# Masked attentions of a fused decoder: division moved ahead of the turn, products with stationary values, scores in two sets of PSUM banks

## What is computed

```python
def fox_attention(hn, w_q, w_o, k, v, c_bhs):          # 16 heads of 64
    """Forgetting attention: logit[t,s] = q_t.k_s/sqrt(d) + c[t] - c[s], s<=t."""
    ...
        s = jnp.where(causal, s + bias, NEG_BIG)
        pr = jax.nn.softmax(s, axis=-1)
        return jnp.einsum("bhqk,bkhd->bqhd", pr.astype(v.dtype), v)
    ...
    return o @ w_o
def moba_attention(q, k, v):                           # 8 heads of 64
    ...
        s_own = (jnp.einsum("bhqd,bhkd->bhqk", qi, k_own) * scale
                 - slopes[..., None] * dist_own)
    ...
        scores = jnp.concatenate([s_sel.reshape(...), s_own], axis=-1)
        p = jax.nn.softmax(scores, axis=-1).astype(v.dtype)
```

## Time and profile before

| | us |
|---|---|
| median of 3 runs | 2239.92 (2239.6 to 2240.91) |
| the profiled execution's own time | 2240.7 |
| its span, first to last instruction | 2238.9 |
| busy: TensorE, VectorE, GpSimd, ScalarE | 2132.1, 1025.5, 936.6, 808.5 |
| mean granted TensorE clock | 0.981 |

### The profile page before, as it was taken

The page is one execution under the profiler, slowest core; times in us unless marked ns, Lnnn a source line. Parts: engine busy times, 40 slices in busy tenths (PEclk is TensorE's granted clock), DMA queues, the critical chain, the costliest instruction groups (busy, mean ns, idle before and its releaser), DMA issues.

```text
span 2238.9 us, 27199 instructions
## 1 busy us (share of the span) xinstructions
PE 2132.1 (95%) x10072; PEld 1750.2 (78%) x10072; DVE 1025.5 (46%) x1632; ACT 808.5 (36%) x1214; POOL 936.6 (42%) x435
## 2 busy tenths in 40 slices
PE   7977999999999988999999998999998999999997
PEld 6765888888878966788888876887877788888885
DVE  7995523122364345352232366248333346354353
ACT  6745422222352156332222354224244243222231
POOL 5974444444444300354444432343331434444441
PEclk9988999999999999999999999999999999999998
DMA  4321332232222310332222221222211222322221
GB/s 183 135 101 58 125 119 94 94 108 90 102 77 94 114 48 30 113 113 94 94 94 94 94 94 40 97 94 76 94 57 39 77 93 95 112 95 94 94 94 57
DMA packets 32204, 205.31 MB, mean 92 GB/s; under 512 B 4448, under 2 KB 4576, under 8 KB 9072
## 3 DMA queue, kind: packets, MB, share of 16 engines
q1 hardware_dynamic: 31824, 199.87, 25.5%
q10 hardware_dynamic: 288, 4.19, 0.5%
HBM read 197.73 MB, written 6.32 MB: 91 GB/s over the span
## 4 chain that ended last, share of the span: by engine, by line
PE 84%; DVE 9%; issue 3%; POOL 2%; ACT 2%; DMA 0%; DVEq 0%; ACTq 0%; POOLq 0%
PE gp L530 26%; PE gp L532 26%; PE gp L531 26%; PE gp L718 2%; DVE ms L1213 2%; PE ms L760 2%; POOL pool_sum L456 1%; PE ms L705 1%; DVE xc L1213 1%; DVE T L1210 1%; DVE U L1683 1%; PE ms L762 0%; DVE T L1565 0%; PE ms L656 0%; PE ms L596 0%
## 5 line engine op out<-in xcount | busy, mean ns | idle before, releaser
L433 POOL TENSOR_TENSOR w_lo<-raw,w_hi 128x1024 fp32r<-128x1024 f32 x350 | 846.6, 2421 | 1198.2 <-ACT w_hi L848 1180.7
L530 PE MATMUL gp<-a_hi,w_hi 128*128 128x512 f32 x1440 | 568.2, 395 | 20.4 <-DVE a_lo L1213 13.1
L531 PE MATMUL gp<-a_lo,w_hi 128*128 128x512 f32 x1440 | 564.2, 392 | 0.0
L532 PE MATMUL gp<-a_hi,w_lo 128*128 128x512 f32 x1440 | 564.1, 392 | 0.0
L848 ACT ACTIVATE w_hi<-raw 128x1024 fp32r<-128x1024 f32 x349 | 365.6, 1051 | 513.4 <-PE gp L532 512.3
L530 PE MATMUL gp<-b_hi,w_hi 128*128 128x512 f32 x1184 | 463.4, 391 | 10.2 <-DVE b_lo L1210 8.4
L531 PE MATMUL gp<-b_lo,w_hi 128*128 128x512 f32 (+1 forms) x1216 | 471.7, 388 | 0.0
L532 PE MATMUL gp<-b_hi,w_lo 128*128 128x512 f32 x1184 | 461.6, 390 | 0.0
L530 PEld LDWEIGHTS gp<-a_hi,w_hi 128*128 128x128 f32 x1440 | 272.7, 189 | 80.8 <-issue 14.8
L531 PEld LDWEIGHTS gp<-a_lo,w_hi 128*128 128x128 f32 x1440 | 272.6, 189 | 58.2 <-issue 1.7
L532 PEld LDWEIGHTS gp<-a_hi,w_lo 128*128 128x128 f32 x1440 | 272.6, 189 | 57.2
(11 more groups left out here) (263 smaller groups left out, 1944.1 us busy)
## 6 DMA issues: line engine op xcount, KB each, us to landing
raw<-w_hbm SPq DMA_DIRECT2D x176, 1024.0 KB, 4.8
proj_scratch<-kT ACTq DMA_DIRECT2D x2, 2048.0 KB, 6.6
fbias<-negc_scratch SPq DMA_DIRECT2D x16, 256.0 KB, 3.5
h<-x_hbm SPq DMA_DIRECT2D x4, 512.0 KB, 7.3
u_pad<-proj_scratch SPq DMA_DIRECT2D x1, 2048.0 KB, 9.7
big<-proj_scratch SPq DMA_DIRECT2D x1, 2048.0 KB, 8.6
out_hbm<-h SPq DMA_DIRECT2D x4, 512.0 KB, 2.7
mem_raw<-mem_hbm SPq DMA_DIRECT2D x1, 1024.0 KB, 12.3
```

What stands on the lines that cost most here:

```text
L433: g.tensor_tensor(at(w_lo), src, f32(at(w_hi)), ALU.subtract).then_inc(w_lo_done, 1)
L530: pe.matmul(o, wh, xh, start=start, stop=False)
L531: pe.matmul(o, wh, xl, start=False, stop=False)
L532: return pe.matmul(o, wl, xh, start=False, stop=stop)
```

## The change

In the masked attentions a pair i takes the place of the step as the grain of TensorE's order: scores of pair i, turns of pair i - 3, products of pair i - 4. Scores go to `ms[:, 0:2]` and `gp[:, 0:2]` in turn, so that they wait for the biases of the pair before the last. The weights have eight places, `prob_of`. VectorE takes both reciprocals of a pair in one instruction, between the pair's two biases, and GpSimd divides the weights by their sums before they are turned. ScalarE copies the first head's turned weights, VectorE the second's. In the products the values are stationary (64 columns) and the turned weights move (128 columns); the heads write partitions 0 to 63 and 64 to 127 of `gp[:, 2 + j % 2]`. The output so stands in its final orientation: the turn of the output and `o_sb` fall away here. TensorE no longer waits for the last remainder behind the attention; `gemm(wo)` has its own waits by k, and `branch(1)` waits before its third slab. In `mob` the wait for banks is reduced to two banks, before the second pair. GpSimd's divides stand in its queue ahead of the slabs of the next gemm, in `mob` with the later two bias products between them. The rest of the diff, left out, is new semaphore counts (`pt`, `pv`, `o`) for the cross attention, which keeps its order.

```diff
@@ -240,6 +240,8 @@
         big = u_pad[:, :, TAPS - 1:]
         bigs, proj_sb = (big, big1), kT
         prob, probT = T, (U[:, 1, :], acc_sq, sqb[:, 0, :], sqb[:, 1, :])
+        prob_of = (T[:, 2, 3 * P:], T[:, 3, 3 * P:], U[:, 0, 0:2 * P], U[:, 0, 2 * P:],
+                   T[:, 2, 0:3 * P], T[:, 3, 0:3 * P], T[:, 0, :], T[:, 1, :])
...
@@ -461,6 +463,13 @@
...
+            def divide(at, s):
+                r, w = s % 8, (s % 8 // 2 + 1) * P
+                g.wait_ge(sum_inv, at["step"] + s + 1)
+                p = prob_of[r][:, 0:w]
+                g.tensor_scalar(p, p, rinv[:, r:r + 1], None, ALU.mult).then_inc(weighted, 1)
...
@@ -477,7 +486,10 @@
             g.wait_ge(hg_done, gate[0]["hg"] + 8)
             g.memset(f32(wf_hi[:]), 0.0).then_inc(wf_zero, 1)
             g.memset(f32(wf_lo[:]), 0.0).then_inc(wf_zero, 1)
-            slabs(gq["slab"] + AHEAD, br[2]["slab"] + AHEAD)
+            slabs(gq["slab"] + AHEAD, wo["slab"] + AHEAD)
+            for s in range(64):
+                divide(fox, s)
+            slabs(wo["slab"] + AHEAD, br[2]["slab"] + AHEAD)
...
@@ -503,8 +515,10 @@
             mob_bias(1)
             for a in range(AHEAD):
                 slab(Pos(br[1]["slab"] + a))
-            mob_bias(2)
-            mob_bias(3)
+            for s in range(32):
+                divide(mob, s)
+                if s in (9, 17):
+                    mob_bias(s // 8 + 1)
             slabs(br[1]["slab"] + AHEAD, ffn2["slab"])
...
-            def head_scores(queries, keys):
-                def scores(j, s):
...
+            def head_attention(at, n, queries, keys, values, before):
...
+                t0, N = at["step"], 4 * n
+                def S_(i):
+                    j, qb = divmod(i, 4)
+                    w, bank = (qb + 1) * P, (ms, gp)[i % 2]
+                    if i == 1:
+                        for c in range(2):
+                            wait_evac(pe, before, c)
+                    if i >= 2:
+                        pe.wait_ge(biased, t0 + 2 * i - 2)
                     for hh in range(2):
                         r = slice(64 * hh, 64 * hh + 64)
-                        pe.matmul(ms[:, hh, 0:w], queries[r, j, qb * P:qb * P + P], keys[r, j, 0:w], start=True, stop=False)
+                        pe.matmul(bank[:, hh, 0:w], queries[r, j, qb * P:qb * P + P], keys[r, j, 0:w], start=True, stop=False)
                     for hh in range(2):
-                        pe.matmul(ms[:, hh, qb * P:w], identb[:], tri[:], start=False, stop=True).then_inc(scored, 1)
-                return scores
-            def head_v(t):
-                def v_of(j, s, kb):
-                    return t[:, kb, j * P + 64 * (s % 2):j * P + 64 * (s % 2) + 64]
-                return v_of
-            attention(fox, 8, biased, [1, 1, 2, 2, 3, 3, 4, 4], head_scores(qT, kT), head_v(v_s), 64, 2, 4)
+                        pe.matmul(bank[:, hh, qb * P:w], identb[:], tri[:], start=False, stop=True).then_inc(scored, 1)
+                def T_(i):
+                    for hh in range(2):
+                        s = 2 * i + hh
+                        pe.wait_ge(weighted, at["weighted"] + s + 1)
+                        if i:
+                            pe.wait_ge((pt_copied, pt_copied2)[hh], at[("pt", "pt2")[hh]] + i)
+                        for kb in range(i % 4 + 1):
+                            m = pe.transpose(ms[:, 2 + hh, kb * P:kb * P + P], prob_of[s % 8][:, kb * P:kb * P + P], ident[:])
+                        m.then_inc(transposed, 1)
+                def V_(i):
+                    j, qb = divmod(i, 4)
+                    pe.wait_ge(pt_copied, at["pt"] + i + 1)
+                    pe.wait_ge(pt_copied2, at["pt2"] + i + 1)
+                    if qb == 0 and j >= 2:
+                        pe.wait_ge(lo_done, at["split"] + j - 1)
+                    for kb in range(qb + 1):
+                        for hh in range(2):
+                            c = j * P + 64 * hh
+                            m = pe.matmul(gp[64 * hh:64 * hh + 64, 2 + j % 2, qb * P:qb * P + P], values[:, kb, c:c + 64],
+                                          probT[(2 * i + hh) % 4][:, kb * P:kb * P + P], start=(kb == 0), stop=(kb == qb),
+                                          skip_group_check=True)
+                    m.then_inc(pv_done, 1)
+                for i in range(N + 4):
+                    if i < N:
+                        S_(i)
+                    if 3 <= i < N + 3:
+                        T_(i - 3)
+                    if i >= 4:
+                        V_(i - 4)
+            head_attention(fox, 8, qT, kT, v_s, Pos(gv["blk"] + 12))
...
-            def branch(n, k0, ysplit, kn):
+            def branch(n, k0, ysplit, kn, late=4):
                 at = br[n]
                 for half in range(2):
                     sl, bl = at["slab"] + 6 * half, at["blk"] + 8 * half
                     for s in range(4):
+                        if s == late and not half:
+                            pe.wait_ge(lo_done, ysplit + kn)
                         slab_ws(Pos(sl + s), Pos(bl + s), A)
                     pe.wait_ge(lo_done, ysplit + kn)
                     for s in range(2):
...
             branch(0, 0, lru["split"], 4)
-            for c in range(4):
-                wait_evac(pe, Pos(br[0]["blk"] + 12), c)
-            attention(mob, 4, biased, [1, 1, 2, 2, 3, 3, 4, 4], head_scores(qm, km), head_v(vm), 64, 2, 4)
-            branch(1, 4, mob["split"], 4)
+            head_attention(mob, 4, qm, km, vm, Pos(br[0]["blk"] + 12))
+            branch(1, 4, mob["split"], 4, late=2)
...
-            def head_exp(s):
...
+            def head_attention(at, X, k0, n):
+                t0, N = at["step"], 4 * n
+                def E_(s):
+                    w = (s % 8 // 2 + 1) * P
+                    act.wait_ge(biased, t0 + s + 1)
+                    p = prob_of[s % 8][:, 0:w]
+                    act.activation(p, p, ACT.Exp, scale=-1.0, bias=nmax[:, s % 8:s % 8 + 1], accum_out=rsum[:, s % 8:s % 8 + 1]
+                                   ).then_inc(exped, 1)
+                def C_(i):
+                    w = (i % 4 + 1) * P
+                    act.wait_ge(transposed, t0 + 2 * i + 1)
+                    if i >= 2:
+                        act.wait_ge(pv_done, at["pv"] + i - 1)
+                    act.activation(probT[2 * i % 4][:, 0:w], ms[:, 2, 0:w], ACT.Copy).then_inc(pt_copied, 1)
+                def H_(j):
+                    act.wait_ge(pv_done, at["pv"] + 4 * (j + 1))
+                    act.activation(X[0][:, k0 + j], gp[:, 2 + j % 2], ACT.Copy).then_inc(hi_done, 1)
+                for i in range(N + 3):
+                    if i >= 3:
+                        C_(i - 3)
+                    if i < N:
+                        E_(2 * i)
+                        E_(2 * i + 1)
+                    if i >= 8 and i % 4 == 0:
+                        H_(i // 4 - 2)
+                H_(n - 1)
+            head_attention(fox, A, 0, 8)
...
-            attention(mob, B, 4, 4, 8, head_exp, causal, STATS, 4)
+            head_attention(mob, B, 4, 4)
...
-            def head_bias(b_of, ready):
-                def bias(j, s):
-                    qb, hh = s // 2, s % 2
+            def head_attention(at, X, k0, n, bias_of, ready):
+                t0, N = at["step"], 4 * n
+                def B_(s):
+                    j, qb, hh = s // 8, s % 8 // 2, s % 2
+                    w = (qb + 1) * P
                     if qb == 0:
                         ready(2 * j + hh)
-                    w = (qb + 1) * P
+                    v.wait_ge(scored, t0 + s + 1)
+                    if s >= 8:
+                        v.wait_ge(transposed, t0 + s - 7)
                     v.sem_inc(step_open, 1)
-                    return v.tensor_tensor_reduce(prob[:, s % 4, 0:w], ms[:, hh, 0:w], b_of(2 * j + hh, qb, w), -1.0, 3e38,
-                                                  ALU.add, ALU.min, nmax[:, s:s + 1])
-                return bias
-            def head_out(s):
-                return s // 2, 64 * (s % 2)
-            attention(fox, A, 0, 8, 8,
-                      head_bias(lambda r, qb, w: fbias[:, r % 4, 0:w], lambda r: v.wait_ge(bias_ready[r % 4], 16 * (r // 4 + 1))),
-                      64, head_out, STATS, 4)
+                    v.tensor_tensor_reduce(prob_of[s % 8][:, 0:w], (ms, gp)[s // 2 % 2][:, hh, 0:w], bias_of(2 * j + hh, qb, w), -1.0, 3e38,
+                                           ALU.add, ALU.min, nmax[:, s % 8:s % 8 + 1]).then_inc(biased, 1)
+                def R_(i):
+                    r = 2 * i % 8
+                    v.wait_ge(exped, t0 + 2 * i + 2)
+                    v.reciprocal(rinv[:, r:r + 2], rsum[:, r:r + 2]).then_inc(sum_inv, 2)
+                def C_(i):
+                    w = (i % 4 + 1) * P
+                    v.wait_ge(transposed, t0 + 2 * i + 2)
+                    if i >= 2:
+                        v.wait_ge(pv_done, at["pv"] + i - 1)
```

(61 more changed lines are left out.)

## The result

The changed kernel takes 2201.31 us (median of 4 runs, 2198.37 to 2202.81), the kernel before 2240.36 beside it: ratio 0.9826, 95% interval 0.9812 to 0.984, so 39 us less. The profiled execution of after is the fastest of its four, 2198.37 us with a span of 2196.6, against 2238.9 before: 42.3 less.

What follows compares the result with a forecast made beforehand. TensorE was taken as the bound, busy 95%, with order and waits costing 2.2 of each 12.87 us attention unit and products 4.5. First attention -28.1, second -15.6, together -43.7 from 2240.7, less 0.8 for the median: 2196 us, range 2187 to 2217.

Steps and rivals of the forecast that it cites:

- the forecast's own case: Whole kernel: products side by side and the change working as meant, 2187 to 2204 us, chance 0.60.
- Products side by side: Masked attentions' products: both heads' column halves stream together, 0.21 a pair of calls, 2.1 us a unit.
- The rival of products in sequence: Masked attentions' products: column halves run one after the other, units of 11.0, 2214 us; chance 0.25.
- TensorE's own work: A unit of two heads, four pairs: scores, masks, turns, products and switches sum to 8.7 us; residue for late hand-overs 0.2.
- VectorE's queue: In a unit: the copy behind both biases holds the next turns, 512 pair 2.95 instead of 2.5, unit 9.2.
- the division on GpSimd: Eight divides a unit: 0.61 to 1.29 for 512 columns, 3.4 to 6.9 us a unit, covered by the lag.
- Divides at the upper end would not lengthen it: In the attention units: even 6.9 us of GpSimd divides would leave the unit at 9.4 us.
- 2.1 us inside that lag: Second attention: two bias products of 1.04 in GpSimd's queue fit in the three pairs' lag (6 us or more).
- the last divides hide behind VectorE's queue: End of both attentions: divides done at 5.6, VectorE's copy only at 6.3; last scores to last products 8.8 us.
- The start: Both attentions: fourth scores at 3.2 us in the first, 4.0 in the second, plus 1.0 each for lost clock.
- The clock behind `mob`: Gemm behind the second attention: granted clock 0.87 over 13 us returns to 1.00, 1.7 us gained.
- The rival of a falling clock: In the attentions: turns and short products with more stops lose the granted clock, 2276 us; chance 0.05.

Runs made afterwards that it cites:

- cheap divides: The changed kernel with GpSimd's divides written as a product of two tensors, the sums' column broadcast; 2190.42 us.
- the order by head: Products of a pair issued with all blocks of the first head ahead of the second's; 2204.22 us on the changed kernel, 2195.26 with the two-tensor divides.
- the experiment on the end's queue order: Against the kernel with two-tensor divides, VectorE's last reciprocal put behind the copy of the pair three before; 2188.66 us.
- the first experiment: GpSimd's divides as a two-tensor product instead of tensor by scalar column, against the changed kernel; 2190.42 us, ratio 0.9779.
- one set of banks: The changed kernel with scores always to the same two banks, each pair waiting for both biases of the pair before; 2212.9 us.
- the old order of the reciprocals: Reciprocals between the next pair's two biases, as in the changed kernel; the run that put them ahead of both took 2197.73 us.

## Why the prediction was right, and where it wasn't

**Right in size, in part by luck:** 2196 against 2201.31, in the range and in the forecast's own case. With cheap divides, nearer to what the prediction assumed, the kernel takes 2190.42, 5.6 under the forecast. So the sum was too long elsewhere, and the slow divides filled what it had too much.

**Products side by side, right.** 0.21 a pair of calls was taken, 0.205 measured. The rival of products in sequence falls in its own terms: even in the order by head the halves overlap in part (+0.69 a unit, not +2.1).

**TensorE's own work, nearly right.** 8.7 was worked out, with a residue 8.9; the kernels with cheap or no divides run at 8.90, or 8.83 where ScalarE does the copies. Mode switches at 0.1 were the nearer end: had each cost 0.22, the sum would be 0.7 higher, 9.4, above both.

**VectorE's queue, wrong.** The 2.95 for the 512 pair assumed that the next turns need VectorE's copy. The first head's turns need ScalarE's alone, and the second head's come later; the pair takes 2.53, in the changed kernel as with cheap divides. What VectorE's copies cost a unit, with cheap divides, is 0.07. Unit 9.37 against 9.4 is therefore a coincidence: the prediction's 9.2 stood on a queue that doesn't bind, and the real 9.37 on divides that it held to be covered. Undoing VectorE's copies (units 9.37 with and without them) shows it.

**The step that failed is the division on GpSimd.** I took 0.61 for 512 columns and bounded it by 1.29; it takes 1.56, outside both ends, 8.7 a unit in place of 3.4 to 6.9 (by width alone the two rows would give 3.1 and 6.5). With it fell two sentences. "Divides at the upper end would not lengthen it" checked the load against the unit, and the load does fit in `fox`; it missed the loop, in which 5.55 of divides lie in series with a turn, scores, a bias and a reciprocal. "2.1 us inside that lag" treated the bias products in `mob` as latency; an engine that is full has no lag to hide them in: units of 10.48 instead of 9.4. At the end I had the last divides hide behind VectorE's queue: the last four take 862.59 to 868.13, and the last turn waits 0.88 for them; 10.53 instead of 8.8, and 8.76 with cheap divides, which the forecast's end had by other steps (the miss of the experiment on the end's queue order speaks against those). What the step costs in all is the first experiment's: 10.9 us of medians, 11.8 by the two stretches.

**The start.** `fox` has no lost clock: 2.84 against 3.2 + 1.0; but its first unit takes 10.76, and together that is 13.60 as against 13.6. That match is luck as well: with cheap divides it is 2.84 + 9.07. `mob`, counted from where the prediction starts it, 0.12 ahead of the first scores: 3.92 + 9.74 = 13.7 against 14.4. The lost clock shows where one set of banks thins the start. So the added 1.0 was wrong here.

**The clock behind `mob`, right:** 0.87 to 1.00, 1.7 us. The run with the wait put back on cheap divides says that the pause alone needn't lower it. Why it fell before and not there isn't shown. The rival of a falling clock didn't come about in the units: 1.00 with 20 turns in each, and the Trainium skill's statement that the full clock doesn't engage for transposes (TensorE: Matmul & The Clock Gate, Part 4, PE-mode transpose) doesn't come out in this trace, after the change as before it; the turns here stand among other matmuls. The drain that the Trainium skill names for a change of tiling mode (TensorEngine Tiling, Key Properties) costs 0.1 to 0.2 a switch here: turns to products 833.29 + 0.22 to 833.61, products to scores 833.61 + 0.82 to 834.64.

**Sum.** `fox` 80.33 against 78.8, `mob`, counted as the prediction did, from the end of the last matmul's stream 0.2 after its start, 45.1 against 42.0: 4.6 short. 3.3 elsewhere, over half of it clock, hides most of that in the profiled run, whose time of 2198.37 is the fastest of four; the median doesn't have it. The three unprofiled runs take 1.6 to 4.4 us more, and their mean granted clock goes with it: 0.984 in the profiled run, then 0.983 (2199.94), 0.981 (2202.81) and 0.981 (2202.67). The profiles show two places where one execution loses clock and another doesn't: 20 to 25 us, 1.7 us, and `fox`'s end, 1.3 us in two of the variants. Which of them the slower runs of after lost isn't shown.

## What to carry to other kernels

An engine that sits idle has a price list of its own: the row of another operation is no price for a new one, so set the upper end well above the slowest row of that engine. Fitting a queue's load under the period isn't enough: follow each result round to the instruction that needs it, and if the path closes on itself within one period, its sum is the period. When a forecast meets the time, read the pace's chain all the same; here two errors gave one right number.

## What the runs showed of the hardware that I had not expected

- On GpSimd the product of a tensor and a column of scalars costs 606, 925, 1244 and 1564 ns for 128, 256, 384 and 512 columns; the same product with the column broadcast as a second tensor costs 401, 614, 827 and 1041. By the rows the one-tensor form is half again as dear.
- Products into the two partition halves of one bank overlap even when all blocks of one head are issued before the other's: 16 in 1.58 us, against 1.09 interleaved. Matmuls of the second half start ahead of earlier ones of the first (834.73 against 834.83).
- At the end of both attentions the kernels with the slow divides and the old order of the reciprocals have the same two waits, 0.40 to 0.41 and 0.88 to 0.89 us, before short turns. There are ten such ends: two each in after, in the products by head, the one set of banks, the copies by ScalarE and the wait behind the attention, all on after. The granted clock fell to 1.2 GHz in two of them, `fox`'s in the last two of these kernels, at a cost of 1.3 us each; the last turns last 1.12 there and 0.66 in the other eight. The same waits don't always have the same clock behind them.
- An execution's time goes with its mean granted clock: the kernel before, in one session, from 2238.38 us at 0.983 to 2244.37 at 0.979.
